# Two pieces of the next expert's weights land beside the ring instead of one

## The reference, cut to what matters

```
h   = rmsnorm(x, g_norm2) * (1 + sc2) + sh2
top 4 of 32 experts for each token, softmax over the four logits
for each expert e and the tokens that chose it:
    gu   = x @ w_gu[e] + b_gu[e]              # 1024 x 2048
    act  = (clip(up) + 1) * min(gate, 7) * sigmoid(1.702 * gate)
    out += weight * (act @ w_down[e] + b_down[e])   # 1024 x 1024
x = x + gt2 * out; final RMSNorm
```

## Time and profile before

| what | value |
|---|---|
| median of three runs | 1624.18 us |
| the profiled execution | 1626.19 us, span 1624.6 us, mean granted clock 0.920 |
| TensorE matmul (PE) | busy 1400.6 us, 86% |
| VectorE, ScalarE, GpSimd | busy 39%, 15%, 11% |
| HBM read | 499.92 MB, 311 GB/s over the span |
| expert part | from about 577 us to 1600 us of the span |
| GpSimd copies, L2259 | 124 of 1041 ns |
| slot selection, L1735 | 168 of 281 ns on average |
| slot weights, L1749 | 55 of 551 ns |

### The profile page before, as it was taken

How to read it: one execution, slowest core, us unless ns; L and a number is a source line. 1 busy time by engine, 2 the same in 40 slices (tenths; PEclk the granted TensorE clock), 3 DMA queues, 4 the chain that set the end, 5 groups by cost and what they waited for, 6 DMA issues and landing times.

```text
span 1624.6 us, 40871 instructions
## 1 busy us (share of the span) xinstructions
PE 1400.6 (86%) x16375; PEld 759.8 (47%) x16376; DVE 630.2 (39%) x1341; ACT 247.6 (15%) x580; POOL 183.8 (11%) x240
## 2 busy tenths in 40 slices
PE   5998989999999689969999796977949978879793
PEld 2445656367676445534555353433414434335352
DVE  2334556443624443433434232422423424224234
ACT  1124532211110311101111010100100101001011
POOL 2011310000000001111011011011011000100000
PEclk8999999988899699989999898988979989889897
DMA  9734992950092459699999999999999997996962
GB/s 355 243 123 162 340 391 103 341 180 1 23 336 108 155 237 413 282 375 402 412 403 396 416 423 402 404 427 414 401 428 418 394 392 292 406 412 272 415 257 96
DMA packets 71426, 505.66 MB, mean 311 GB/s; under 512 B 6528, under 2 KB 6648, under 8 KB 35316
## 3 DMA queue, kind: packets, MB, share of 16 engines
q1 hardware_dynamic: 63588, 480.98, 73.7%
q0 software_dynamic: 7792, 24.08, 4.5%
HBM read 499.92 MB, written 5.11 MB: 311 GB/s over the span
## 4 chain that ended last, share of the span: by engine, by line
PE 69%; DMA 20%; DVE 6%; issue 2%; ACT 1%; POOL 1%; SPq 1%; DVEq 0%; ACTq 0%; POOLq 0%
PE psum L544 63%; DMA region<-in_w_gu 12%; DMA ring<-in_w_down 6%; DMA ring<-in_w_ada 2%; PE psum L708 2%; PE psum L1038 1%; PE psum L1013 1%; DVE region L1335 1%; POOL ring L2259 1%; DMA ring<-in_w_gu 1%; DVE region L1184 1%; PE psum L740 0%; ACT region L1870 0%; DVE region L1302 0%; SPq L2324 0%
## 5 line engine op out<-in xcount | busy, mean ns | idle before, releaser
L544 PE MATMUL psum<-ring,region 128*32 128x256 f32 (+2 forms) x11264 | 742.5, 388 | 132.0 <-POOL ring L2259 126.0
L544 PEld LDWEIGHTS psum<-ring,region 128*32 128x32 f32 (+1 forms) x11264 | 370.2, 112 | 452.9 <-POOL ring L2259 154.9
L1870 ACT ACTIVATE region<-psum 128x256 f32<-128x256 f32 (+5 forms) x330 | 136.7, 417 | 1144.9 <-PE psum L544 509.3
L544 PE MATMUL psum<-region 128*32 128x256 f32 (+11 forms) x2708 | 254.3, 424 | 20.1 <-DVE region L1228 9.0
L2259 POOL COPY ring<-region 128x1024 f32<-128x1024 f32 x124 | 123.7, 1041 | 933.3 <-DMA region<-in_w_gu 723.9
L1779 DVE TENSOR_TENSOR region<-region,psum 128x1280 f32<-128x1280 f32 x110 | 163.3, 1485 | 166.2 <-PE psum L544 166.2
L544 PE MATMUL psum<-region,ring 128*128 128x320 f32 (+1 forms) x640 | 170.4, 421 | 1.5 <-DVE region L1590 1.4
L1749 DVE TENSOR_SCALAR region<-psum,region 128x320 f32<-128x320 f32 x55 | 30.3, 551 | 357.6 <-PE psum L544 357.6
L544 PEld LDWEIGHTS psum<-region 128*32 128x32 f32 (+6 forms) x2708 | 102.5, 138 | 130.2 <-issue 91.7
L544 PEld LDWEIGHTS psum<-region,ring 128*128 128x128 f32 x640 | 117.9, 194 | 48.6 <-issue 5.4
L1735 DVE TENSOR_SCALAR region<-region 128x32 f32<-128x32 f32 x168 | 37.2, 281 | 92.8 <-issue 92.8
(11 more groups left out here) (321 smaller groups left out, 771.1 us busy)
## 6 DMA issues: line engine op xcount, KB each, us to landing
ring<-in_w_gu SPq DMA_DIRECT2D x97, 2048.0 KB, 11.2
ring<-in_w_down SPq DMA_DIRECT2D x64, 2048.0 KB, 11.4
region<-in_w_gu SPq DMA_DIRECT2D x31, 2048.0 KB, 17.5
ring<-in_w_ada SPq DMA_DIRECT2D x12, 2048.0 KB, 13.6
ring<-in_w_in SPq DMA_DIRECT2D x11, 2048.0 KB, 19.0
ring<-in_cache_k SPq DMA_DIRECT2D x64, 256.0 KB, 5.1
ring<-in_cache_v POOLq DMA_DIRECT2D x64, 256.0 KB, 5.3
ring<-in_w_out SPq DMA_DIRECT2D x2, 2048.0 KB, 22.6
```

The costliest lines, as they stand in the source:

```text
L544: return pe.matmul(out, lhsT, rhs, start=start, stop=stop, skip_group_check=True)
L1870: return act.activation(out, src, ACT.Copy)
```

## The change: a second landing, for unit 5

The landings are now listed by unit (`LANDED_APART = (0, 5,)`). A second landing is laid over routing scratch that is dead by then; tiles that live on (`pos`, `wts`, `plan_row` and the final ones) are moved out of its way. For each expert SP now issues units 1, 2, 3, 4, then unit 0 of the next expert into landing 0, then unit 5 of the next expert into landing 1. GpSimd copies unit 0 and then unit 5 into the ring, four pieces each. `down` waits for unit 5's four pieces instead of for its DMA. Before the loop SP waits for the drained `bd` banks and for a new semaphore that VectorE raises after the split of the weights, and fills landing 1 for expert 1.

```diff
-LANDINGS = 1
+LANDED_APART = (0, 5,)
+LANDINGS = len(LANDED_APART)
...
+        landing = [region[:, REGION + KT * NT - UNIT:REGION + KT * NT], Area(E.at).take(UNIT)]
         logits = E.take(3, NE)
         mask = E.take(3, NE)
...
             def down(expert):
                 for half in range(2):
                     i = 4 + half
-                    pe.wait_ge(unit_landed[moe_slot[i]], 16 * expert + (landed_base[i] + 16))
+                    if i in LANDED_APART:
+                        pe.wait_ge(piece_moved[LANDED_APART.index(i)], PIECES * expert + PIECES)
+                    else:
+                        pe.wait_ge(unit_landed[moe_slot[i]], 16 * expert + (landed_base[i] + 16))
...
                     step(dve.tensor_tensor(rest, rest, place_weight[0:rows - NE, :], ALU.subtract))
+            dve.tensor_copy(plan_row[0:1, 0:1], plan_row[0:1, 1:2]).then_inc(weight_rows_ready, 1)
             for m in range(KT):
                 dve.wait_ge(*drained("bd", m))
...
-                for i in range(LANDINGS):
-                    pool.wait_ge(unit_landed[moe_slot[i]], landed_base[i] + 16)
-                    pool.wait_ge(unit_read[i], before)
+                for i, n in enumerate(LANDED_APART):
+                    pool.wait_ge(unit_landed[moe_slot[n]], landed_base[n] + 16)
+                    pool.wait_ge(unit_read[n], before)
                     pool.wait_ge(landing_filled[i], filled)
                     for piece in range(PIECES):
                         part = slice(UNIT // PIECES * piece, UNIT // PIECES * (piece + 1))
-                        pool.tensor_copy(ring[:, moe_slot[i], part], landing[i][:, part])\
+                        pool.tensor_copy(ring[:, moe_slot[n], part], landing[i][:, part])\
                             .then_inc(piece_moved[i], 1)
...
             def expert_weights(expert, blocks_before):
                 for i in range(RING):
                     if blocks_before is None:
                         sp.wait_ge(*last_use[units[len(units) - RING + i][0]])
-                    elif i < LANDINGS:
+                    elif i in LANDED_APART:
                         continue
...
             expert_weights(slice(0, 1), None)
             sp.wait_ge(*full("h2", 2, 1))
             fill_landing(0, slice(1, 2))
             sp.wait_ge(tables, 1)
+            for m in range(KT):
+                sp.wait_ge(*drained("bd", m))
+            sp.wait_ge(weight_rows_ready, 1)
+            fill_landing(1, slice(1, 2))
             with sp.Fori(1, NE - 1) as e:
```

More of the change, by code:

```diff
@@ L268, in build @@
         selwT = E.take(NT)
+        pos = E.take(3, ROUNDS * NE)
         E.at = max(E.at, fin_at + KT * NT + 2 * FF)
         late_const = E.take(n_const - n_late)
+        wts = E.take(3, NE)
+        fin_ss = E.take(6)
+        fin_rstd = E.take(3)
+        plan_row = E.take(N_LIST)
+        fin_gain = E.take(D)
+        landing = [region[:, REGION + KT * NT - UNIT:REGION + KT * NT], Area(E.at).take(UNIT)]
         logits = E.take(3, NE)
         mask = E.take(3, NE)
-        wts = E.take(3, NE)
         eq = E.take(3, NE)
@@ L295, in build @@
         reached = E.take(3, NE)
[L296 to L299, removed]
         x1_sq = Area(REGION - KT * NT).take(KT, NT)
-        landing = [region[:, REGION + KT * NT - UNIT:REGION + KT * NT]]
         assert E.at <= REGION - KT * NT
-        pos = E.take(3, ROUNDS * NE)
+        assert E.at <= REGION + KT * NT - UNIT
         y_out = h2_tok
@@ L391, in build @@
         bias_in = sem("bias_in")
+        weight_rows_ready = sem("weight_rows_ready")
         landing_filled = [sem(f"landing_filled{i}") for i in range(LANDINGS)]
@@ L1021, in gate_up_quarter @@
             def gate_up_quarter(c, expert):
-                if c >= LANDINGS:
+                if c not in LANDED_APART:
                     pe.wait_ge(unit_landed[moe_slot[c]], 16 * expert + (landed_base[c] + 16))
@@ L1027, in gate_up_quarter @@
                     for q, out_bank in ((0, B_GATE), (1, B_UP)):
-                        if c < LANDINGS:
-                            pe.wait_ge(piece_moved[c], PIECES * expert + (2 * j + q + 1))
+                        if c in LANDED_APART:
+                            pe.wait_ge(piece_moved[LANDED_APART.index(c)], PIECES * expert + (2 * j + q + 1))
                         last = spread(out_bank, hgT[:, j, LANES[c]],
@@ L2302, in _, with send_unit @@
             dn = I["w_down"].rearrange("e (h c p j) f -> e h p c (j f)", h=2, c=2, j=2)
+            def send_unit(i, expert, dst):
+                if i < 4:
+                    src = gu[expert, i].rearrange("o p f -> p (o f)")
+                else:
+                    src = dn[expert, i - 4].rearrange("o p c f -> p (o c) f")
+                    dst = dst.rearrange("p (c f) -> p c f", c=2)
+                return sp.dma_start(dst, src)
             def fill_landing(i, expert):
-                sp.dma_start(landing[i], gu[expert, i].rearrange("o p f -> p (o f)")).then_inc(landing_filled[i], 16)
+                send_unit(LANDED_APART[i], expert, landing[i]).then_inc(landing_filled[i], 16)
             def expert_weights(expert, blocks_before):
@@ L2316, in expert_weights @@
                         sp.wait_ge(unit_read[i], blocks_before)
[L2318 to L2324, removed]
+                    send_unit(i, expert, ring[:, moe_slot[i], :]).then_inc(unit_landed[moe_slot[i]], 16)
             expert_weights(slice(0, 1), None)
```

## The result

| | before | after |
|---|---|---|
| median of the runs, us | 1624.97 (1618.1 to 1633.33, 20 runs) | 1633.12 (1628.36 to 1639.7, 20 runs) |
| ratio to before | 1 | 1.0048, 95% interval 1.0036 to 1.006 |
| span of the profiled execution, us | 1624.6 | 1631.5 |
| mean granted clock | 0.920 | 0.917 |

The account below looks back on a forecast made before the run. Bound: a loop of TensorE's reads, SP's issues and DMA's weight transfers. Passed-on stalls +12.5, w_down -1.3, start +0.3, end -1.1 sum to +10.4 us, a median of 1634.6; 8-in-10 range 1613 to 1643 us.

Parts of the forecast that it names:

- The pauses: Four DMA pauses of 10.8 us, in the last block of each three-block expert: unchanged, no gain (bounds 0 and 19.7 us).
- The start: Before the loop, SP's three added waits delay unit 1 of expert 1: 0.3 us later (bounds 0 and 4.93).
- w_down: TensorE's waits for unit 5 from 600 to 1580 us go: 1.3 us earlier.
- The stalls: First stall of 12.14 us becomes 7.2 plus a second wait of 3.9; quarter 1 starts 0.7 us earlier per stall.
- The clock: Clock falls in the second wait, slowing quarter 1 and `down`: 2.0 us lost per stall (bounds 0 and 2.8).
- The rival with the clock up: Clock stays up after the second wait, ten stretches gain 0.7 us each: -9.1 us, 1615.1 us; chance 0.17.
- What is passed on: Net 1.25 us later per stall, passed on in ten stretches from stall to stall: +12.5 us.
- the one stretch that was held too full to pass anything on: 1189 to 1219 us, DMA at 425 GB/s, the fullest: a microsecond lost or won by TensorE does not move later work.
- The end: Last expert has no unit 5 to fetch after unit 4, so the last half's 1.12 us wait goes: 1.1 us earlier.
- GpSimd, SP, VectorE at nothing: Four added copies per expert, 4.0 us, and SP's new wait cost 0 (bounds 0 and one copy, 1.04 us, each).
- The mean clock: Mean granted clock over the execution near 0.905, by 11 x 4 us more at half.

Follow-up runs that it names:

- The filled waits: Changed kernel with unread matmuls before quarter 1 in the stalled blocks: 1628.81 us with a loop in every block, 1615.11 us with a branch to the stalled ones.
- The kernel with the branch: Changed kernel plus 8 rounds of unread matmuls before quarter 1, reached by a branch in the stalled blocks only: 1615.11 us, 0.992 of the kernel before.
- the filled kernel: Changed kernel plus unread matmuls before quarter 1, by a loop: 1 + 8 rounds in the stalled blocks, 1 in all others: 1628.81 us, 1.0041 of the kernel before.
- its control: Changed kernel plus the same loop of unread matmuls before quarter 1, with 1 round in every block: 1646.5 us, 1.0148 of the kernel before.

## Why the prediction was right

The direction, the mechanism and most sizes held; 1634.6 us was forecast, 1633.12 measured. Step by step:

- **The pauses.** No gain, as said, and the count of units holds; but they are 0.2 to 2.0 us longer than the 10.8 us that were to stay.
- **The start, and w_down.** 0.3 us later was said. Quarter 1 of expert 1 begins at 593.66 us, and its unit had landed at 593.80 before: nothing was lost. The wait for w_down is gone, as said, and the first pause ends 0.5 us earlier.
- **The stalls.** 6.70 us where 7.2 was said, and a second wait of 4.45 where 3.9 was said; over all eleven 70.9 us, 6.4 each, and the new ones 4.0 to 4.7 us.
- **The clock.** The term was 2.0 us per stall; quarter 1 and `down` take 7.25 us on average where they took 5.50: 1.75 us. The low time in them is 3.8 us on average, 4.2 was taken; the extremes are 2.7 and 5.6. The filled waits agree: 17.7 to 21 us over eleven stalls is 1.6 to 1.9 each. The rival with the clock up was given 1615.1 us, and the kernel that holds it up took 1615.11. That this fits to the hundredth is luck: by its ratio that kernel gains 13 us (9.8 to 16.1) on the kernel before, and the rival had 9.1.
- **What is passed on.** Net 1.25 us per stretch was said, +12.5; from 0.5 to 9.3 us over the ten stretches between the stalls is 0.88 each, +8.8. This is the term that was too large. The kernel with the branch splits it. At the end of quarter 1 it is 0.1 us behind the kernel before at the first stall and 10.1 ahead at the last: without the clock the change wins 1.0 us per stretch, and 0.83 (0.7 and 0.13) was in the sum. Against the changed kernel it goes from 0.4 to 19.5 us ahead: the clock costs 1.9 us per stretch, and 2.1 was in the sum. The loss is not even, either: the first five stretches add 1.2 us together, the last five 7.7; why is open. And the one stretch that was held too full to pass anything on, from 1189 us, added 1.5 us, so that exception did not hold.
- **The end.** -1.1 us was said. The lag falls from 9.3 us at the last stall to 6.9 at the end of the span, so by 2.4, and 1.3 of it where the wait was: the last two halves of the loop's end now run through as one group, with the wait for ScalarE that was to stay and without that for w_down:

```profile
1597.77 3.66 PE L547 MATMUL psum<-ring,region 128*32 128x256 f32 x64 [0.47 <-ACT region L1877]
```

- **GpSimd, SP, VectorE at nothing.** Unit 1 was due at about 716 us and was issued at 715.63. The selections beside copies went from 281 to 290 ns on average (168 of them, 1.5 us in all). No wait of TensorE for VectorE appeared.
- **The mean clock** was to be near 0.905 and is 0.917. Eleven times 4 us of low time were added, but the shorter first wait took low time away that cost nothing. From 720 to 733.7 us, in the first stall, before and then after:

```profile
720.00:733.70 13.70, 4.57 (x34) 0.51 1.01 429
```
```profile
720.00:733.70 13.70, 6.08 (x54) 0.62 1.02 434
```

The Trainium skill, "TensorE: Matmul & The Clock Gate" (Part 1: The HAM clock gate), has the ramp at less than 1% of a typical kernel's span. Here the falls in eleven short waits cost 17.7 us, 1.1%, by the filled kernel and its control; the interval of that difference, about 14 to 21 us, doesn't tell it from 1%. Taken as a bound, it would have given +4.3 us (an estimate) where +8.1 was measured and +10.4 forecast.

## What to carry to other kernels

Between two units that a stalled engine wants one behind the other, a prefetched third one is a second wait: order transfers by need where they set the pace, and run ahead only where the engine does. A sum of waits can fall while the time rises; look at what runs behind each wait, and at which clock. Waits that can't be removed can be filled, if the filling is shorter than the wait and its branch stands behind enough work of the engine to cost nothing.

## What was not expected of the hardware

A value load and a branch on TensorE cost nothing visible behind the transposes (quarter 1 starts 0.43 us after them with the branch and 0.44 without), but 0.75 us of idle time ahead of quarter 0, where the bias rows before it take 0.40 us. That these are too short to cover it is a reading that was not tried by itself. And four GpSimd copies of 128x256 in one stretch took 1.43 us, 0.36 each, more than a quarter of the 1.0 us that 128x1024 take.
